# A transformer layer with routed experts: expert rows added in memory by the indirect transfer instead of stored and summed at the end

## The reference

```python
v = _rmsnorm(h, g_ffn)
logits = v @ w_router + b_router                 # 32 experts
top_val, top_idx = top_k(logits, 4)
gates = softmax(top_val)                         # over the 4 chosen
# for each token t and each of its 4 experts e:
#   a = v[t] @ w_mlp1[e] + b_mlp1[e]             # 1024 -> 2048
#   y = clamped_swiglu(a) @ w_mlp2[e] + b_mlp2[e]
h[t] += gate * y                                 # summed over the 4 experts
```

## Time and profile before

| | us |
|---|---|
| median of three runs | 2607.39 |
| the profiled execution's own time | 2607.83 |
| its span | 2606.2 |
| router stage, about 741 to 902 | 161 |
| expert stage, about 902 to 2535 | 1633 |
| last stage, 2535 to the end | 71 |

### The profile page before, as it was taken

The page is one execution under the profiler, slowest core; times in us unless marked ns, Lnnn a source line. Parts: engine busy times, 40 slices in busy tenths (PEclk is TensorE's granted clock), DMA queues, the critical chain, the costliest instruction groups (busy, mean ns, idle before and its releaser), DMA issues. The chain is left out here.

```text
span 2606.2 us, 35142 instructions
## 1 busy us (share of the span) xinstructions
PE 2335.1 (90%) x10673; PEld 1742.3 (67%) x10674; DVE 1924.8 (74%) x2425; ACT 1451.3 (56%) x1694; POOL 477.3 (18%) x546
## 2 busy tenths in 40 slices
PE   6999698999979579999899889999999999988964
PEld 5767565555558457777778677777777777777741
DVE  4699456999956368787775687777777777788767
ACT  4222355888832166676654475656565567667540
POOL 0466100111102311221110011212121111122120
PEclk9999798999989789999999899999999999999985
DMA  4233712332016398797976688877887679799868
GB/s 155 59 108 94 161 40 80 66 66 50 17 45 114 93 337 324 282 348 271 360 254 223 236 318 294 305 256 267 287 311 261 240 277 356 260 353 360 293 242 361
DMA packets 259924, 574.86 MB, mean 221 GB/s; under 512 B 29201, under 2 KB 61329, under 8 KB 254721
## 3 DMA queue, kind: packets, MB, share of 16 engines
q1 hardware_dynamic: 237296, 534.92, 60.3%
q0 software_dynamic: 21056, 34.49, 3.7%
q10 hardware_dynamic: 1488, 4.39, 0.4%
HBM read 548.17 MB, written 60.15 MB: 233 GB/s over the span
## 5 line engine op out<-in xcount | busy, mean ns | idle before, releaser
L1732 DVE TENSOR_TENSOR wlo<-raw,whi 128x2048 fp32r<-128x2048 f32 x387 | 880.6, 2287 | 293.2 <-ACT whi L1628 285.9
L1628 ACT CAST whi<-raw 128x2048 fp32r<-128x2048 f32 x387 | 730.9, 1909 | 227.1 <-PE gl_ps L1900 138.5
L1902 PE MATMUL gl_ps<-whi,xt_hi 128*128 128x512 f32 x1056 | 420.9, 399 | 41.6 <-PEq L1946 24.6
L1904 PE MATMUL gl_ps<-whi,xt_lo 128*128 128x512 f32 x1056 | 414.3, 392 | 0.0
L1903 PE MATMUL gl_ps<-wlo,xt_hi 128*128 128x512 f32 x1056 | 414.1, 392 | 0.0
L1902 PEld LDWEIGHTS gl_ps<-whi,xt_hi 128*128 128x128 f32 x1056 | 199.9, 189 | 93.6 <-issue 25.5
L1904 PEld LDWEIGHTS gl_ps<-whi,xt_lo 128*128 128x128 f32 x1056 | 200.1, 190 | 43.3
L1903 PEld LDWEIGHTS gl_ps<-wlo,xt_hi 128*128 128x128 f32 x1056 | 200.4, 190 | 40.1
L1902 PE MATMUL y_ps<-whi,ht_hi 128*128 128x512 f32 x512 | 215.2, 420 | 0.0
L1903 PE MATMUL y_ps<-wlo,ht_hi 128*128 128x512 f32 x512 | 208.7, 408 | 0.0
L1904 PE MATMUL y_ps<-whi,ht_lo 128*128 128x512 f32 x512 | 208.3, 407 | 0.0
(11 more groups left out here) (262 smaller groups left out, 3954.3 us busy)
## 6 DMA issues: line engine op xcount, KB each, us to landing
raw<-in_w_mlp SPq DMA_DIRECT2D x390, 1024.0 KB, 6.1
b<-in_b_mlp SPq DMA_DIRECT2D x33, 1024.0 KB, 7.7
yk<-y_dram SPq DMA_DIRECT2D x7, 2048.0 KB, 24.7
k_st<-qk_dram SPq DMA_DIRECT2D x32, 260.0 KB, 7.5
xs<-in_x SPq DMA_DIRECT2D x16, 512.0 KB, 4.6
w_in_raw<-in_w_in SPq DMA_DIRECT2D x32, 256.0 KB, 2.9
q_st<-qk_dram SPq DMA_DIRECT2D x32, 256.0 KB, 6.7
qk_dram<-qk_hi SPq DMA_DIRECT2D x24, 256.0 KB, 2.6
```

The lines of the kernel that those rows point to most:

```text
L1628: act.copy(whi[:, k % SPL, :], raw[:, k % RAW, :]).then_inc(hi_done, 1)
L1732: dve.tensor_tensor(wlo[:, k % SPL, :], raw[:, k % RAW, :], whi[:, k % SPL, :].bitcast(F32), ALU.subtract).then_inc(lo_done, 1)
L1902: pe.matmul(bank, xh[:, half, kc, :], hi, start=start, stop=False, skip_group_check=True)
L1904: return pe.matmul(bank, xl[:, half, kc, :], hi, start=False, stop=stop, skip_group_check=True)
```

## The change

The residual rows now go to `sum_dram`, which has 256 spare rows behind the 1024. The code of a pair is now the token's number and the bits of its gate; both gather and store go by the token's number. The two stores of a job carry an add: each row of `ys` is read, the row of `sum_dram` is read, and the sum is written there. Since rows are added, they must be weighted before: ACT's copy from PSUM gets the gate as its scale, and the rows of a few-job are multiplied on VectorE. Unused places carry the numbers 1024 to 1279 and gate 0, so that each goes to a spare row of its own (the gathers still skip them, the stores don't). The spare rows are filled from the input by one transfer from memory to memory. For the gates to be there when the codes are written, subtraction, exponential, reciprocal and product move into each tile's turn, with the sum taken by the exponential. `combine` loads only `sum_dram`, adds the bias part and stores.

```diff
@@ route, POOL
-            pool.memset(none[:, :], SEQ * TOP_K).then_inc(ready, 1)
-            pool.iota(code[:, :, :, 0], pattern=[[P * TOP_K, NT], [1, TOP_K]], base=0, channel_multiplier=TOP_K
-                      ).then_inc(codes_set, 1)
-            pool.iota(code[:, :, :, 1], pattern=[[P, NT], [0, TOP_K]], base=0, channel_multiplier=1
-                      ).then_inc(codes_set, 1)
+            pool.memset(none[:, :, 1], 0).then_inc(ready, 1)
+            pool.iota(none[:, :, 0], pattern=[[1, JOB]], base=SEQ, channel_multiplier=0).then_inc(ready, 1)
+            pool.iota(code[:, :, :, 0], pattern=[[P, NT], [0, TOP_K]], base=0, channel_multiplier=1).then_inc(codes_set, 1)
...
+            pool.dma_start(sum_dram[SEQ:SEQ + JOB, :], a["x"][0, 0:JOB, :]).then_inc(cleared, 16)
@@ route, ACT
-            act.wait_ge(gates_in, 1)
-            act.activation(gates[:, :, :], gates[:, :, :], ACT.Exp).then_inc(gates_exp, 1)
+                if t >= 1:
+                    u = t - 1
+                    act.wait_ge(gates_in, u + 1)
+                    act.activation(gates[:, u, :], gates[:, u, :], ACT.Exp, accum_out=gsum[:, u:u + 1]).then_inc(gates_exp, 1)
@@ route, DVE, choose(u)
                 step(dve.max(top[:, u, :], lg[:, :]))
+                dve.tensor_tensor(gates[:, u, :], top[:, u, 0:TOP_K], top[:, u, 0:1].broadcast_to((P, TOP_K)), ALU.subtract
+                                  ).then_inc(gates_in, 1)
@@ route, DVE, place(u)
+                dve.wait_ge(gates_exp, u + 1)
+                step(dve.reciprocal(gsum[:, u:u + 1], gsum[:, u:u + 1]))
+                step(dve.tensor_scalar(gates[:, u, :], gates[:, u, :], gsum[:, u:u + 1], None, ALU.mult))
+                step(dve.tensor_copy(code[:, u, :, 1].bitcast(F32), gates[:, u, :]))
                 dve.wait_ge(rank_ready, u + 1)
@@ experts, POOL
+            def keep(to, of, done):
+
+                pool.tensor_copy(to[:, :, 0], of[:, :, 0]).then_inc(done, 1)
+                pool.tensor_copy(to[:, :, 1].bitcast(F32), of[:, :, 1].bitcast(F32)).then_inc(done, 1)
...
-                pool.tensor_copy(idm[:, :], idn[:, :, 0]).then_inc(idx_held, 1)
+                keep(idm, idn, idx_held)
...
-                    pool.indirect_dma_start(out=y_dram[:, :],
-                                            out_offset=bass.IndirectOffsetOnAxis(ap=idc[:, half:half + 1], axis=0),
-                                            in_=ys[:, half, :], in_offset=None,
-                                            bounds_check=SEQ * TOP_K - 1, oob_is_err=False).then_inc(y_stored[half], 16)
+                    pool.indirect_dma_start(out=sum_dram[:, :],
+                                            out_offset=bass.IndirectOffsetOnAxis(ap=idc[:, half, 0:1], axis=0),
+                                            in_=ys[:, half, :], in_offset=None, bounds_check=SEQ + JOB - 1,
+                                            oob_is_err=True, compute_op=ALU.add).then_inc(y_stored[half], 16)
...
-                pool.tensor_copy(idc[:, :], idm[:, :]).then_inc(idx_kept, 1)
+                keep(idc, idm, idx_kept)
@@ experts, ACT, finish
-                    ins = act.copy(ys[:, half, 512 * q:512 * q + 512], src)
+                    ins = act.activation(ys[:, half, 512 * q:512 * q + 512], src, ACT.Copy,
+                                         scale=idc[:, half, 1:2].bitcast(F32))
@@ experts, DVE, few_finish
                 dve.wait_ge(gf_in, j * 6 + 7)
-                dve.sem_inc(y_out[1], 1)
+                dve.wait_ge(idx_kept, j * 2 + 2)
+                dve.tensor_scalar(ys[0:FEW, 1, :], ys[0:FEW, 1, :], idc[0:FEW, 1, 1:2].bitcast(F32), None, ALU.mult
+                                  ).then_inc(y_out[1], 1)
@@ combine
-            eng.dma_start(h2[:, t, n0:n1], h2_dram[t * P:(t + 1) * P, n0:n1]).then_inc(y_sem[i], 16)
-            eng.dma_start(yk[:, t, :, n0:n1], rows[:, :, n0:n1]).then_inc(y_sem[i], 16)
+            eng.dma_start(h2[:, t, n0:n1], sum_dram[t * P:(t + 1) * P, n0:n1]).then_inc(y_sem[i], 16)
...
-                for k in range(TOP_K):
-                    if k:
-                        dve.wait_ge(added, TOP_K * i + k)
-                    else:
-                        dve.wait_ge(based, i + 1)
-                    dve.scalar_tensor_tensor(out=h2[:, t, n0:n1], in0=yk[:, t, k, n0:n1], scalar=gates[:, t, k:k + 1],
-                                             in1=h2[:, t, n0:n1], op0=ALU.mult, op1=ALU.add).then_inc(added, 1)
```

More of the change, by code:

```diff
@@ L1055, in _, with route @@
                     act.copy(ot[:, u % 2, :], o_ps[0:DV, :]).then_inc(ot_done, 1)
-def route(nc, a, mixed, gates, jobs, chosen, h2_dram, v_dram, slot_dram, weights):
+def route(nc, a, mixed, gates, jobs, chosen, sum_dram, v_dram, slot_dram, weights):
     with ExitStack() as ctx:
@@ L1092, in route @@
         code = sb("code", [P, NT, TOP_K, 2], U32)
-        none = sb("none", [P, N_EXP * CAP * 2 // P], U32)
+        none = sb("none", [P, JOB, 2], U32)
         gsum = sb("gsum", [P, NT])
@@ L1305, in _ @@
                     choose(t - 1)
[L1307 to L1312, removed]
             step(dve.memset(ec[:, :], 1.0))
@@ L1424, in _, with experts @@
             pe.matmul(r_ps[0:1, 128 + 2 * NJ:128 + 3 * NJ], ec[:, 2:3], ej[:, 2, :], start=True, stop=True).then_inc(cnt_ready, 1)
-def experts(nc, a, jobs, v_dram, slot_dram, y_dram):
+def experts(nc, a, jobs, v_dram, slot_dram, sum_dram):
     with ExitStack() as ctx:
@@ L1454, in experts @@
         idn = sb("idn", [P, 2, 2], U32)
-        idm = sb("idm", [P, 2], U32)
-        idc = sb("idc", [P, 2], U32)
+        idm = sb("idm", [P, 2, 2], U32)
+        idc = sb("idc", [P, 2, 2], U32)
         ident = sb("ident5", [P, P])
@@ L1562, in gather @@
                 pool.indirect_dma_start(out=xg[:, half, :], out_offset=None, in_=v_dram[:, :],
-                                        in_offset=bass.IndirectOffsetOnAxis(ap=idn[:, half, 1:2], axis=0),
+                                        in_offset=bass.IndirectOffsetOnAxis(ap=idn[:, half, 0:1], axis=0),
                                         bounds_check=SEQ - 1, oob_is_err=False).then_inc(x_landed[half], 16)
+            def keep(to, of, done):
+                pool.tensor_copy(to[:, :, 0], of[:, :, 0]).then_inc(done, 1)
+                pool.tensor_copy(to[:, :, 1].bitcast(F32), of[:, :, 1].bitcast(F32)).then_inc(done, 1)
             load_idx(0)
@@ L1573, in _ @@
             pool.wait_ge(setup, 2)
-            pool.tensor_copy(idc[:, :], idn[:, :, 0]).then_inc(idx_kept, 1)
+            keep(idc, idn, idx_kept)
             for half in range(2):
                 pool.wait_ge(x_landed[half], 16)
-            pool.wait_ge(idx_kept, 1)
+            pool.wait_ge(idx_kept, 2)
             load_idx(1)
@@ L1663, in finish @@
                 await_bank(act, j, NP - 1, half, kind)
-                act.wait_ge(idx_kept, j + 1)
+                act.wait_ge(idx_kept, j * 2 + 2)
                 if half and kind == "few":
@@ L1985, in _, with combine @@
                 turn(pe, body, j)
-def combine(nc, a, gates, chosen, h2_dram, y_dram, out):
+def combine(nc, a, gates, chosen, sum_dram, out):
     with ExitStack() as ctx:
@@ L2005, in combine @@
         y_sem = [sem(f"yk_landed{i}") for i in range(NQ)]
-        o_sem, added, dense_done = sem("out_stored"), sem("added"), sem("dense_done")
+        o_sem, dense_done = sem("out_stored"), sem("dense_done")
         small_in, gt_ready, gt_copied, b_ready = sem("small_landed"), sem("gates_turned"), sem("gates_copied"), sem("b_ready")
@@ L2012, in load @@
             t, n0, n1 = pieces[i]
-            rows = y_dram[t * P * TOP_K:(t + 1) * P * TOP_K, :].rearrange("(p k) d -> p k d", k=TOP_K)
-            eng.dma_start(h2[:, t, n0:n1], h2_dram[t * P:(t + 1) * P, n0:n1]).then_inc(y_sem[i], 16)
-            eng.dma_start(yk[:, t, :, n0:n1], rows[:, :, n0:n1]).then_inc(y_sem[i], 16)
+            eng.dma_start(h2[:, t, n0:n1], sum_dram[t * P:(t + 1) * P, n0:n1]).then_inc(y_sem[i], 16)
         @block.sync
@@ L2028, in _ @@
             for i, (t, n0, n1) in enumerate(pieces):
-                act.wait_ge(y_sem[i], 32)
-                act.wait_ge(added, TOP_K * (i + 1))
+                act.wait_ge(y_sem[i], 16)
+                act.wait_ge(based, i + 1)
                 act.dma_start(out[0, t * P:(t + 1) * P, n0:n1], h2[:, t, n0:n1]).then_inc(o_sem, 16)
@@ L2061, in _ @@
             for i, (t, n0, n1) in enumerate(pieces):
-                dve.wait_ge(y_sem[i], 32)
+                dve.wait_ge(y_sem[i], 16)
                 dve.wait_ge(b_ready, t + 1)
@@ L2093, in build @@
                 attend_diff(nc, a, v_all, mixed, qk_dram, stacks, weights)
-            route(nc, a, mixed, gates, jobs, chosen, h2_dram, v_dram, slot_dram, weights)
-        experts(nc, a, jobs, v_dram, slot_dram, y_dram)
-        combine(nc, a, gates, chosen, h2_dram, y_dram, out)
+            route(nc, a, mixed, gates, jobs, chosen, sum_dram, v_dram, slot_dram, weights)
```

(2 more changed lines are left out.)

19 lines of the change are left out of this document (9 added, 10 removed).

## The result

The changed kernel takes 2578.11 us (median of 4 runs, 2577.52 to 2579.32) against 2608.2 for the kernel before beside it (4 runs, 2606.91 to 2609.14): a ratio of 0.9886, 95% interval 0.9868 to 0.9903. Forecast were 2584.3 us in a range of 2573 to 2610, faster with a chance of 0.80. It is faster, by 30 us, and 6 us faster than forecast. The profiled execution took 2577.95 us, its span 2576.3.

What follows compares the result with a forecast made beforehand. VectorE's additions were taken to bound the last stage, with TensorE busy 94% of the expert stage. Span 2606.2 - 31.3 + 1.0 + 4 + 3.2 = 2583.1 us, as median of runs 2584.3, range 2573 to 2610.

Steps and rivals of the forecast that it cites:

- The last stage: Last stage: scaled additions go, TensorE's bias products of 27.9 us become the chain; a gain of 31.3 us, bounds 27 and 32.
- The identity: Last stage: the identity matrix was to land 4.5 us after its issue in place of 8.8.
- Rival C: Last stage: TensorE gets 2.4 GHz, products take 14 us instead of 27.9; some 12 us less, 2572; chance 0.05.
- The price of the adding transfer: Expert stage's stores: double the plain price, 188 us in place of 47, +4.4 us a job.
- twice the megabytes and about four times the share: Queue 0 of the DMA engines: what its traffic would show if the prediction was right.
- The expert stage: Expert stage: one-jobs want 43.6 us of DMA in 40, felt only in four in a row; +4, bounds 0 and 130.
- a lead of 8 us: Expert stage: with six weight buffers, TensorE feels a DMA deficit only beyond some 8 us.
- Rival A: Expert stage: adding transfer makes DMA the bound; +130 at four times plain price, decides at 2.7; in full 0.12, partial 0.08.
- Rival B: Price plain or hidden everywhere: expert stage loses nothing, end 1.5 us, identity lands at 3.5; 2578; chance 0.16.
- The router stage: Router stage: a table load and subtractions go on the path in the last two turns; net +1.0 us, bounds 0 and 3.
- The end: Behind the last job: nothing hides the last store, now 128 rows; +3.2 us, bounds 1.5 and 8.
- Rival D: Expert stage: weighting or copies delay the next job, 27 us return, 2611; chance 0.07 together with a price near 2.7.

Runs made afterwards that it cites:

- The first experiment: The kernel before, with its last stage neither loading nor adding the expert rows: 2576.45 us, ratio 0.9888.
- the plain store: The changed kernel with the add taken out of its indirect stores, all 128 rows still written: 2583.29 us, ratio 0.9915; run again, 2580.17 us, ratio 0.9905.
- The smaller copy: The changed kernel with a further memory-to-memory copy of 1.5 MB on SP's queue in each job: 2594.07 us, ratio 0.9954.
- the larger: The changed kernel with 3 MB more copied from memory to memory on SP's queue in each job: 2643.65 us, ratio 1.0137.
- split operands: The changed kernel with gates and bias split into high and low parts, stacked on 96 rows for the bias products: 2565.37 us; run again, 2563.88 us.

## Why the prediction was right, and where it was not

**The last stage: right in mechanism and size.** The identity landed 6.15 us after its issue, not 4.5; the products took 27.68 us, forecast 27.9; from their end it was 3.9 us to the end of the span (2572.36 to 2576.3), forecast 4.0. The whole is 41.2 for 39.7, and the difference is the identity. The first experiment shows by itself that this stage is the gain. Rival C, the full clock, did not come: the granted clock is 0.50 through the stage, also with 27.7 us of unbroken products.

**The price of the adding transfer: right.** 327 ns against 159 for a packet of 4 KB is 2.06 times, and queue 0's share of 9.2% of 2576 us is 237 us of all engines against 96 before: +141, as forecast (188 less 47). Of the 141, the plain store with all rows makes 41 (its share is 5.3%) and the add 100. The Trainium skill, page Collectives: The Full Stack, section The bandwidth ceiling, says that an add in the DMA engines has two sources to read and so half the rate. The ratio of 2.06 agrees with it; that both are read through one ring no run here shows. The sign named for this, "twice the megabytes and about four times the share" on queue 0, fits the stores alone: the queue also carries the gathers, and went from 34.49 to 52.30 MB and from 3.7% to 9.2%, as the forecast's own sum of +141 us would have given.

**The expert stage: this term failed.** "I take +4 for the stage" rested on "a one-job wants 39.2 + 4.4 = 43.6 us of DMA in 40" and on a run of four one-jobs that would exceed a lead of 8 us. The run of four, from its first store at 2255.79 to the one at 2420.77, took 164.98 us and between 2257.98 and 2422.84 before 164.86. Before, then after:

```profile
2257.98 1.01 POOL L1602 DMA_INDIRECT y_dram<-ys,idc  x1 [17.47 <-ACT ys L1672]
...
2422.84 1.01 POOL L1602 DMA_INDIRECT y_dram<-ys,idc  x1 [12.80 <-ACT ys L1672]
```

```profile
2255.79 1.61 POOL L1608 DMA_INDIRECT sum_dram<-ys,idc  x1 [17.61 <-ACT ys L1678]
...
2420.77 1.61 POOL L1608 DMA_INDIRECT sum_dram<-ys,idc  x1 [8.68 <-ACT ys L1678]
```

A few-job took 56.9 us (2198.86 to 2255.79) against 57.0. With the clock taken into account the whole stage lost nothing that can be told. The step that failed is the adding of shares. The one-job shows 40.6 us of DMA time in its 39 (the share of 1.04), not 43.6; the whole stage +101 us, although queue 0 alone rose by 134 in it. The other queues' packets became shorter: those of 4 KB on queue 1 from a mean of 188 ns to 177, and to 171 and 160 with the two copies, while their median stayed at 159 in all four. I read this so: part of a busy share near one is packets waiting, and it gives way when something else wants the engines. No run takes waiting and moving apart. The plain store shows the same: a share of 0.83, nearly that of before, with all 8192 rows written.

**Rival A: far from true, and its point of decision was mis-set.** It was to decide at 2.7 times the plain price, +130 at four. By the forecast one more plain price is 94 us of packet time (2.9 us a job). The smaller copy's own packets take 119 us, so it stands for a price of some 3.3 times in place of 2, and it cost 15 us; the larger, 261 us, for some 4.8 times, and it cost 65. The point at which the gain of 27 us over its group's kernel before is gone lies between them, at some 3.6 times, an estimate on the line between the two, from copies by SP and not from a dearer adding store. Rival B, that the price is hidden in the stage, came true there, and my 2578 for it is the measured time, but by luck: it had the end at 1.5 us, which is B's plain price and was 3.4, and the identity at 3.5, which was 6.15, and the clock gave about as much back.

**The router stage: right in kind, too small.** +1.0 was forecast; the first cast came 1.6 us later in the profiled execution, and the stage itself is 2.4 us longer (168.4 to 170.9), inside the bounds of 0 and 3; over all executions it is 1 to 4 us. The table load in the last turns is shown to be on the path, 1.28 us in the turn read. The full turns do not add to it: the cast of the transposed tile that the earlier trace rows have at 833.85 is at 833.03. The rest of the 2.4 us was not taken apart.

**The end: right.** +3.2 forecast, 3.4 measured (9.1 to 12.5), 2.6 to 3.0 in the other executions. It takes both the add and the empty rows: with all rows stored plainly the stretch is 10.3 us (+1.2, in both executions), with the add on rows that hold a token alone 9.5 (+0.4).

**Rival D: wrong.** VectorE's multiplication and POOL's copies are in the trace and delay no job; POOL lost 8 of its 12.76 us of room.

**Sum.** Span 2606.2 - 29.8 (last stage) + 3.4 (end) + 1.6 (first cast) - 5.1 (first cast to last store) = 2576.3. The -5.1 is not a gain of the change: the profile of before has 97.5 us at 1.2 GHz in this stage and that of after 88.2, and less half of it the stages differ by 0.4 us. So of the 6 us by which the forecast was too high, the 4 for the stage are a failed step of the working and the rest is the clock, less what the identity and the router stage took more than forecast.

## What to carry to other kernels

A busy share of the DMA engines near one is not proof that they are the bound: add a known amount of traffic and see what it costs, or look whether any consumer waits for a load; here the first 101 us of engine time on top of 1320 were not felt and the next 95 cost 17. When a stage differs by a few us between two kernels, look first how long each was granted the lower clock. When one engine's work is taken out of a stage, work out the next engine's chain to the end and whether its operation has a cheaper form; here that was worth half as much again as the change. And what is hidden inside a loop of jobs stands open once, behind the last job: price it there apart.

## What the runs showed of the hardware

- An indirect transfer that adds took 327 ns for a packet of 4 KB against 159 plain (medians of queue 0), its instruction 1.61 us on POOL against 1.01.
- The mean busy share of the DMA engines went to 1.04 in one-jobs (380 GB/s), and packets of the same queue and size became shorter as load was added beside them (means 188, 177, 171, 160 ns, median 159 throughout).
- The same expert stage took 1603.5 to 1609.3 us from one execution to another, with 85 to 100 us of it at 1.2 GHz.
- TensorE stayed at 1.2 GHz through the whole last stage in every version looked at (0.50 for 41 us here, 28 us with split operands); a float32 product of 32 rows took four records of 0.865 us for a tile of 128 tokens and 1024 values, the split form on 96 rows two of 0.52.
